# Two blocks of a transformer on one core: router, experts and overflow branch in one program, and two norms from one pass

## The reference, cut to what matters

```python
h = rmsnorm(x, norm_ffn) * (1 + scale_f) + shift_f
x = x + gate_f * hierarchical_moe(h, ...)     # 4 groups of 8 experts
x = rmsnorm(x, norm_final)                    # end of the first block
h = rms_norm(x, norm_mix_g) * (1 + sc1) + sh1 # start of the second

def hierarchical_moe(h, ...):
    g_logits = tok @ w_rg + b_rg              # best group, its softmax weight
    e_logits = tok @ w_re + b_re              # two best experts in that group
    combine = ...                             # weight of each expert for each token
    for e in range(32):
        hid = silu(tok @ w_gate[e]) * (tok @ w_up[e])
        out = out + combine[:, e:e + 1] * (hid @ w_down[e])
```

## Time and profile before

| | us |
|---|---|
| median of 3 runs | 1687.56 (1687.36 to 1689.58) |
| the profiled execution | 1686.78 |
| its span | 1685.1 |
| TensorE busy | 1523.9 (90%) |
| VectorE busy | 620.3 (37%) |
| ScalarE busy | 271.5 (16%) |
| GpSimd busy | 233.7 (14%) |
| mean granted clock of TensorE | 0.943 |
| moved by DMA | 352.37 MB |

### The profile page before, as it was taken

The page is one execution under the profiler, slowest core; times in us unless marked ns, Lnnn a source line. Parts: engine busy times, 40 slices in busy tenths (PEclk is TensorE's granted clock), DMA queues, the critical chain, the costliest instruction groups (busy, mean ns, idle before and its releaser), DMA issues. The chain is left out here.

```text
span 1685.1 us, 19200 instructions
## 1 busy us (share of the span) xinstructions
PE 1523.9 (90%) x7873; PEld 1168.5 (69%) x7873; DVE 620.3 (37%) x1089; ACT 271.5 (16%) x563; POOL 233.7 (14%) x305
## 2 busy tenths in 40 slices
PE   2999999498787489989999999899999998999997
PEld 2776775366454178867888888777776887777774
DVE  5577371522121245674445211233322962100002
ACT  1210120110000121121235300100001272100001
POOL 5054000000000110053344500300000000000000
PEclk7998998699999779999999999899999999999999
DMA  9874440499999847684675444788844411344440
GB/s 340 317 269 144 150 150 1 205 413 417 415 416 417 279 128 252 211 298 146 161 189 144 130 148 152 286 307 304 299 150 125 150 51 50 124 151 149 149 149 25
DMA packets 171998, 352.37 MB, mean 209 GB/s; under 512 B 6889, under 2 KB 134048, under 8 KB 154512
## 3 DMA queue, kind: packets, MB, share of 16 engines
q1 hardware_dynamic: 162784, 310.73, 51.5%
q0 software_dynamic: 9136, 40.55, 7.9%
HBM read 350.09 MB, written 1.16 MB: 208 GB/s over the span
## 5 line engine op out<-in xcount | busy, mean ns | idle before, releaser
L2368 PE MATMUL PS<-HT,ring 128*128 128x256 f32 x1616 | 352.5, 379 | 0.0
L2368 PEld LDWEIGHTS PS<-HT,ring 128*128 128x128 f32 x1616 | 307.0, 190 | 49.4 <-issue 8.6
L1688 PE MATMUL PS<-HT,ring 128*128 128x256 f32 x1152 | 265.5, 389 | 2.9 <-PEq L1546 2.9
L1688 PEld LDWEIGHTS PS<-HT,ring 128*128 128x128 f32 x1152 | 220.6, 194 | 40.1 <-issue 10.4
L2674 DVE TENSOR_TENSOR hid<-PS,silu 128x512 f32<-128x512 f32 x22 | 15.2, 692 | 359.0 <-PE PS L2368 359.0
L2384 PE MATMUL PS<-ring,hid 128*128 128x512 f32 x320 | 140.6, 592 | 0.0
L2384 PEld LDWEIGHTS PS<-ring,hid 128*128 128x128 f32 x320 | 60.8, 190 | 68.0 <-issue 67.0
L1847 PE MATMUL PS<-ring,y_T 128*128 128x256 f32 x384 | 83.3, 379 | 0.0
L1847 PEld LDWEIGHTS PS<-ring,y_T 128*128 128x128 f32 x384 | 72.9, 190 | 9.9
L2559 ACT ACTIVATE silu<-PS 128x512 f32<-128x512 f32 x22 | 13.1, 597 | 394.4 <-PE PS L2368 394.4
L426 DVE TENSOR_TENSOR expert_sums<-expert_sums,PS 128x1024 f32<-128x1024 f32 x16 | 19.5, 1222 | 139.9 <-PE PS L374 139.9
(11 more groups left out here) (528 smaller groups left out, 1852.3 us busy)
## 6 DMA issues: line engine op xcount, KB each, us to landing
ring<-in_hy_w_in SPq DMA_DIRECT2D x40, 1024.0 KB, 7.1
ada_stage<-in_ada_w POOLq DMA_DIRECT2D x24, 1024.0 KB, 5.9
ring<-in_ffn_w_gate SPq DMA_DIRECT2D x22, 1024.0 KB, 5.4
ring<-in_ffn_w_up SPq DMA_DIRECT2D x22, 1024.0 KB, 5.3
ring<-in_ffn_w_down SPq DMA_DIRECT2D x22, 1024.0 KB, 4.8
ring_extra<-in_expert_w_up SPq DMA_DIRECT2D x20, 1024.0 KB, 23.3
ring_extra<-in_expert_w_down SPq DMA_DIRECT2D x20, 1024.0 KB, 25.1
ring_extra<-in_expert_w_gate SPq DMA_DIRECT2D x20, 1024.0 KB, 19.9
```

Source lines behind the costliest of these rows:

```text
L1688: mm = pe.matmul(dst, w[:, k, half * P:(half + 1) * P], HT[:, k, :], start=(k == 0), stop=(k == KT - 1))
L2368: mm = pe.matmul(dst, w[:, k, m * P:(m + 1) * P], HT[:, k, :], start=(k == 0), stop=(k == KT - 1))
```

## The change

It merges the programs 3 to 7 into one and the norms of 8 into mixer 2's program, and it reorders the work in them.

- `clear_phase_sems` goes. GpSimd clears the semaphores of a phase in the program of the next one.
- SP runs RING items ahead of mixer 1 to its end; the merged program issues the final norm's gain (into `gate_a`) and then the other items.
- The router takes its logits from X before the norm: X is transposed, multiplied by router weights with the scale in them, then the reciprocal root is applied to the logits, and the product of shift and weights is added to the bias. Squares, root and the scaled rows `xn` are made beside that; HT with normed rows is not made any more (only in the overflow branch).
- `pick` is made for quad 0 first, the rest while TensorE gathers; turning `heavy` moves behind the gate products of quad 0.
- The rows of the experts are multiplied by `gate_b` as they leave PSUM (`gate_rows`, VectorE), and `add` adds to X. The last quad's scatter is cut in four pieces in four banks. `expert_sums` and the two products behind it go.
- The overflow branch stands at the end of the same program behind a flag that each engine loads.
- Four unused ScalarE operations on a few words (`idle`) name the function that is wanted next.
- Norms: `xg` = X times gain. The squares of X and of `xg` are summed one after the other and both roots are taken at once; rows are scaled once for mixer 2, and X is rescaled behind that. The transposes and evictions go to banks 4 to 7 in mixer 2's own program, and its first matmuls wait for one block each.
- `gate_a` is loaded later by GpSimd, behind its small loads and the clearing.

```diff
-    def clear_phase_sems():
-
-        with nc.Block() as block:
-            @block.gpsimd
-            def _(pool):
-                for _, s in phase_sems:
-                    pool.sem_clear(s)
-        for scope, _ in reversed(phase_sems):
+    def retire_sems():
+
+        old = list(phase_sems)
+        phase_sems.clear()
+        return old
+
+    def clear_retired(pool, old):
+        for _, s in old:
+            pool.sem_clear(s)
+
+    def release_sems(old):
+        for scope, _ in reversed(old):
             scope.close()
...
-                    send_until(sp, min(s + 1, segs["moe"].base - RING))
+                    send_until(sp, s + 1)
...
             @block.sync
             def _(sp):
-                send_until(sp, segs["moe"].base, RING + EXTRA)
+                sp.dma_start(fg[:], t["norm_final"].partition_broadcast(P)).then_inc(fg_in, 16)
+                send_until(sp, base, RING + EXTRA)
+                send_until(sp, segs["hy_x"].base)
...
             def _(pe):
-                pe.wait_ge(r_small, 96)
-                for i in range(TT):
-                    for k in range(KT):
-                        mm = pe.matmul(PS[:, i, 0:NR], HT[:, k, i * P:(i + 1) * P], wr[:, k, :],
+                for b in range(4):
+                    for i in range(TT):
+                        for k in (2 * b, 2 * b + 1):
+                            mm = pe.transpose(PS[:, 4 + b, (k % 2) * S + i * P:(k % 2) * S + (i + 1) * P],
+                                              X[:, i, :].rearrange("p (m k) -> p k m", k=KT)[:, k, :], ident[:])
+                    mm.then_inc(x_turned, 1)
...
+                pe.wait_ge(wr_ok, 1)
+                for k in range(KT):
+                    if k % 2 == 0 and k < 4:
+                        pe.wait_ge(xt_dve, k // 2 + 1)
+                    elif k % 2 == 0:
+                        pe.wait_ge(xt_act, k // 2 - 1)
+                    for i in range(TT):
+                        mm = pe.matmul(PS[:, i, 0:NR], XR[:, k, i * P:(i + 1) * P], wr_s[:, k, :],
                                        start=(k == 0), stop=(k == KT - 1))
-                mm.then_inc(lgm, 1)
+                mm.then_inc(made, 1)
+                pe.wait_ge(wr_ok, 2)
+                pe.matmul(PS[:, 2, 0:NR], ones[:], shift_sum[:], start=True, stop=True).then_inc(made, 1)
...
+                pe.wait_ge(normed, TT)
+                pe.wait_ge(picked, 1)
+                gather(0, 0)
+                gather(0, 1)
                 for q in range(QUADS):
-                    if q >= 4:
-                        pe.wait_ge(moved, q - 3)
+                    pe.wait_ge(hs_ready, q * 2 + 2)
+                    up_gate(0, q)
+                    if q:
+                        scatter(0, q - 1)
+                    else:
+                        pe.wait_ge(heavied, TT)
+                        turn_heavy()
+                    up_gate(1, q)
+                    if q:
+                        scatter(1, q - 1)
+                    if q < QUADS - 1:
+                        pe.wait_ge(picked, 2)
+                        gather(q + 1, 0)
+                    turn(q)
+                    if q < QUADS - 1:
+                        gather(q + 1, 1)
+                    if q == 0:
+                        pe.wait_ge(put_mv, QUADS)
+                    down(q)
+                pe.wait_ge(y_moved, QUADS)
+                pe.wait_ge(added, FINAL)
+                for i, h, bank in LAST_PIECES:
+                    pe.matmul(PS[:, bank, :], put[:, QUADS - 1, i * P:(i + 1) * P], ys[:, h * 512:(h + 1) * 512],
+                              start=True, stop=True).then_inc(scattered, 1)
...
+                act.activation(idle[:, 0:1], ident[:, 0:1], ACT.Sqrt)
+                for i in range(TT):
+                    act.activation(xn[:, i, :], X[:, i, :], ACT.Square, accum_out=stat[:, i:i + 1]).then_inc(squared, 1)
+                for b in range(2, 4):
+                    act.wait_ge(x_turned, b + 1)
+                    act.activation(XR[:, 2 * b:2 * b + 2, :], PS[:, 4 + b, :].rearrange("p (a n) -> p a n", a=2), ACT.Copy)\
+                        .then_inc(xt_act, 1)
+                act.wait_ge(meaned, 1)
+                act.activation(stat[:, 4:6], stat[:, 2:4], ACT.Sqrt).then_inc(rooted, 1)
+                act.activation(idle[:, 1:2], ident[:, 0:1], ACT.Exp)
...
+                dve.tensor_tensor(wr_s, wr[:], bc(scale, 2, NR), ALU.mult).then_inc(wr_ok, 1)
+                for b in range(2):
+                    dve.wait_ge(x_turned, b + 1)
+                    dve.tensor_copy(XR[:, 2 * b:2 * b + 2, :], PS[:, 4 + b, :].rearrange("p (a n) -> p a n", a=2))\
+                        .then_inc(xt_dve, 1)
+                step(dve.tensor_tensor(wr_t, wr[:], bc(shift, 2, NR), ALU.mult))
+                dve.tensor_reduce(shift_sum[:], wr_t.rearrange("p k n -> p n k"), AX.X, ALU.add).then_inc(wr_ok, 1)
+                dve.wait_ge(squared, TT)
+                dve.tensor_scalar(stat[:, 2:4], stat[:, 0:2], 1.0 / D, EPS, ALU.mult, ALU.add).then_inc(meaned, 1)
+                dve.wait_ge(rooted, 1)
+                step(dve.reciprocal(stat[:, 6:8], stat[:, 4:6]))
+                for i in range(TT):
+                    dve.tensor_scalar(xn[:, i, :], X[:, i, :], stat[:, 6 + i:7 + i], None, ALU.mult).then_inc(normed, 1)
+                dve.wait_ge(made, BIAS)
+                step(dve.tensor_tensor(br[:], br[:], PS[:, 2, 0:NR], ALU.add))
+                for i in range(TT):
+                    ins = dve.scalar_tensor_tensor(out=lg[:, i, :], in0=PS[:, i, 0:NR], scalar=stat[:, 6 + i:7 + i],
+                                                   in1=br[:], op0=ALU.mult, op1=ALU.add)
+                step(ins)
...
+                def choose(e0, e1):
+                    n = e1 - e0
+                    for i in range(TT):
+                        ins = dve.tensor_tensor(pick[:, i, e0:e1, :], bc(place[:, i, e0:e1], 2, SLOTS), bc(slot_no[:], 1, n),
+                                                ALU.is_equal)
+                    ins.then_inc(picked, 1)
+
+                choose(0, QUAD)
                 step(dve.tensor_reduce(most[:, 0:1], PS[:, 3, 0:EXPERTS], AX.X, ALU.max))
                 step(dve.tensor_scalar(most[:, 1:2], most[:, 0:1], float(SLOTS), None, ALU.is_gt))
-                dve.tensor_copy(some_left[:], most[:, 1:2])
+                dve.tensor_copy(some_left[:], most[:, 1:2]).then_inc(left, 1)
+                choose(QUAD, EXPERTS)
...
+                def gate_rows(q):
+                    dve.wait_ge(used, item(q, "d", QUAD - 1) + 1)
+                    dve.tensor_tensor(ys, PS[:, 4:6, :].rearrange("p b n -> p (b n)"), gate_b[:], ALU.mult)\
+                        .then_inc(y_moved, 1)
+
+                def add(h, q):
+                    dve.wait_ge(scattered, q * 2 + h + 1)
+                    part = X[:, :, h * 512:(h + 1) * 512]
+                    dve.tensor_tensor(part, part, PS[:, 6:8, :], ALU.add).then_inc(added, 1)
...
+                make_rows(0)
+                dve.wait_ge(picked, 2)
                 for i in range(TT):
-                    step(dve.tensor_tensor(pick[:, i], bc(place[:, i, :], 2, SLOTS), bc(slot_no[:], 1, EXPERTS),
-                                           ALU.is_equal))
                     dve.tensor_tensor(heavy[:, i], pick[:, i], bc(em[:, i, :], 2, SLOTS), ALU.mult).then_inc(heavied, 1)
-                dve.wait_ge(lgm, 2)
-                dve.tensor_copy(rest[:], PS[0:EXPERTS, 0, 0:S])
-        route.close()
-        sums = sb(scope, "expert_sums", [P, TT, D])
-        routed_experts(pick, put, xn, sums)
-        held.close()
-        overflow_experts(rest, rows_dram, some_left, sums)
-        with nc.Block() as block:
-            @block.vector
-            def _(dve):
-                step = stepper(dve, dve_step)
-                step(dve.tensor_tensor(sums[:], sums[:], bc(gate_b[:], 1, TT), ALU.mult))
-                dve.tensor_tensor(X[:], X[:], sums[:], ALU.add)
+                step(dve.tensor_scalar(keep[:], place[:], float(SLOTS), None, ALU.is_ge))
+                dve.tensor_tensor(keep[:], keep[:], em[:], ALU.mult)
+                for q in range(QUADS):
+                    if q:
+                        add(0, q - 1)
+                        add(1, q - 1)
+                    activate(q)
+                    if q < QUADS - 1:
+                        make_rows(q + 1)
+                    gate_rows(q)
+                dve.wait_ge(added, FINAL)
+                for n, (i, h, bank) in enumerate(LAST_PIECES):
+                    dve.wait_ge(scattered, FINAL + n + 1)
+                    part = X[:, i, h * 512:(h + 1) * 512]
+                    ins = dve.tensor_tensor(part, part, PS[:, bank, :], ALU.add)
+                ins.then_inc(go, 1)
...
+                clear_retired(pool, retired)
+                pool.wait_ge(left, 1)
+                with if_some(pool):
...
+                        if s == 0 and q < 2:
+                            if k < KT // 2:
```

(42 more changed lines are left out.)

572 lines of the change are left out of this document (233 added, 339 removed).

## The result

The changed kernel takes **1650.16 us** (median of 4, 1645.73 to 1653.31), the kernel before 1688.57 in the same session (1687.36 to 1691.79): ratio 0.9768, 95% interval 0.974 to 0.9796. The forecast was 1654, with a range of 1646 to 1663. The profiled execution took 1651.4 us with a span of 1649.4, against 1686.78: 35.4 us less, where the sum of the terms was 33.1.

What follows compares the result with a forecast made beforehand. The expert stage was taken as bound by its weight stream, restarted when the router lets quad 0's gate products end. 18.3 + 9.1 + 3.0 + 3.0 - 0.3 = 33.1 us off 1686.78 gave 1653.7, forecast 1654, range 1646 to 1663.

Steps and rivals of the forecast that it cites:

- up to the start of the merged program: Mixer 1: early items share SP's queue with the last two modulation fetches; 0.3 us lost, 2.5 at worst.
- shift of the stage: Expert stage: earlier gate products of quad 0 let the weight stream flow from 338.5 instead of 356.8; 18.3 us gained.
- tail, from its end: From the last down product's end to the next program's first square: 7.9 us instead of 17.0; 9.1 gained.
- first operation to scaled rows: Norms ahead of mixer 2: first square to scaled rows takes 5.3 us instead of 8.3; 3.0 gained.
- scaled rows to in-projection, and what follows up to 575 us: Mixer 2's start: first in-projection matmul 2.8 us earlier, plus 0.2 for the clock; 3.0 gained.
- second hole: Expert stage: rival that a later down(0) starves the stream again; 1657 at 6 us late, chance 0.07.
- 14.7 later: Router: issue of item 16, after quad 0's gate products, follows the gather's start by 14.7 us, as before.
- 1.5 us for a slow clock: Gather behind a cold stretch of TensorE: taken as 1.5 us slower, bounds 0 and 2.
- 335 at most: Weight stream: first 16 items and the final gain are in by 335 us at most; then it stands still.
- The rival had a tenth: Behind 600 us: a stall of VectorE, ScalarE and GpSimd at about 725 us loses gain; 1660, chance 0.10.
- slower than reckoned: Router: rival that TensorE's clock stays at half through the logits and the gather is at its bound; 1657, chance 0.15.
- The rival of more than reckoned: Gather at full rate, load behind the add, blocks without a gap: 1651, or 1647 if clock stays up; chance 0.10.

Runs made afterwards that it cites:

- the run with the clearing: Changed kernel with the two clearings of semaphores back in programs of their own, all engines waiting: 1660.0 us, ratio 0.9832.
- an execution of the kernel before with the same mixer 2: Kernel before with only SP's limit in mixer 1 lifted, so six expert items are fetched early: 1688.68 us, ratio 1.0001.
- one with the short router: Changed kernel without the square root named ahead of the overflow branch, so both ways leave Silu's table: 1647.63 us, ratio 0.9754.
- the kernel with the adds spread: Changed kernel with the sixteen adds of the modulation sums one in a step, instead of two in some steps: 1638.58 us, ratio 0.9703.
- the root named in mixer 2: Changed kernel with an unused square root at the head of ScalarE's list in mixer 2's program, ahead of the squares: 1645.09 us, ratio 0.9746.

## Why the prediction was right, and where its terms were off

The kernel is faster by what the forecast named, but the sum is closer than its terms. By the spans of the profiled pair, in us:

| term | forecast | measured |
|---|---|---|
| up to the start of the merged program | -0.3 | 1.9 |
| shift of the stage | 18.3 | 23.3 |
| last down product | 0 | 0.3 |
| tail, from its end | 9.1 | 10.4 |
| first operation to scaled rows | 3.0 | 0.8 |
| scaled rows to in-projection, and what follows up to 575 us | 3.0 | 6.0 |
| mixer 2, up to 1060 us | 0 | -9.2 |
| behind it | 0 | 2.2 |
| sum | 33.1 | 35.7 |

The two times differ by 35.4. At 575 us the lead was 42.7 us, nearly ten more than forecast; that the profiled pair came within 3 us of the forecast at its end is luck, as mixer 2 gave 9.2 back in that execution. The medians are 38.4 apart, and 41.2 in the last session.

- **Shift of the stage.** The mechanism was right in each point: the gate products of quad 0 set the restart (the run with the clearing: 7.8 us at item 16, 7.7 at the last down product), the early items only have to be early enough, and no second hole came. The size was off: TensorE's work up to item 16 is 5.4 us shorter than reckoned. Of that, 2.2 lie ahead of the gather (transposes and logits), 1.5 are the gather and 1.7 the gate products, 3.67 from their start to the issue instead of the 5.36 that lay in the "14.7 later" carried over from before (5.20 in the run with the clearing). For transposes and gate products it is the clock, at 1.00 in the changed kernel and at 0.50 for much of them before; I had taken it for the transposes' own pace that they took 3.67. For the gather it isn't: I charged 1.5 us for a slow clock, the clock was slow (0.50 for over four us), and it cost nothing. And the stream was done with its 16 items 30 us after the start and not 33, the forecast's "335 at most", so that it hardly had to wait.
- **Tail.** 1.3 us more than the 9.1. The last adds follow each other at 0.86 us (546.00, 546.86), and from the last one's end to the next program there are 0.7 us, where the forecast had 1.75 for flag, jump and border: 1.0 of the 1.3. The flag's load is hidden, which the forecast had left open. Its pieces up to the last add (1.3 + 4.0 + 0.69) also sum to 6.0 and not to the 6.1 that it gives; 5.9 were measured.
- **Norm.** Right in the arithmetic (5.4 without loads), wrong in the sum: the forecast put the table loads at nothing and didn't ask which table ScalarE holds behind a branch. Two loads of 1.28 us cost 2.1, and 0.8 of the 3.0 us were won.
- **First matmuls.** 7.2 became 4.3, as forecast (4.4). The clock gave 1.8 us, not the 0.2 that I took out of 1.5 at most: 40 records in 8.80 us, 10.56 before.
- **Is anything lost behind 600 us?** The rival had a tenth, and the profiled pair looked like it, with 9.2 us given back. It isn't a fixed loss by the change: an execution of the kernel before with the same mixer 2 loses nearly as much, and one with the short router loses 0.2. The medians, 38.4 us apart, speak against it too. A loss of up to 3 us isn't excluded. The forecast also missed a stall: its "only short stall" before 1053 us, 5.1 us, has a second one beside it in the trace of before, 1.1 us for `rows_q`, and both grew in the profile of the changed kernel.
- **The other rivals.** The clock was at 0.50 in the first part of the gather, but no work in the router's stretches was slower than reckoned. The rival of more than reckoned (1651) came nearest to the median: the load hides behind the add, the gather costs nothing more, and the clock stays up from mixer 1.

What is not settled: why the clock falls where it does, why the gather doesn't feel it, why two executions of one kernel wait 1 or 5 us for `rows_q`, and what part of the 1.9 us ahead of the merged program is the change's; 2.7 us were there at 186 us, ahead of every edit, and are the execution's.

## What to carry to other kernels

A prefetch and the release of its slots are one term: alone the early items were worth nothing, with the short router 8 to 10 us. A pause between programs can cost its length and then the lower clock of what follows (3.8 us and 3.4 more in the run with the clearing), so a step's duration taken from behind a pause isn't the step's own. If one way through a branch ends with another ScalarE table than the other, loads stand behind it; end both with the same one. Before a loss in a stretch that wasn't edited is explained, look at a second execution of the old kernel there: one trace of each can differ by more than the effect.

## What the runs showed of the hardware

- A border of 1.78 us of rest left TensorE's clock at 1.00, and 16 transposes took 2.04 us; after a rest of 5.58 us it was 0.50, and they took 3.65. The length of the rest alone doesn't decide: in the kernel before, a rest of 1.83 us ahead of the logits, behind only 3.68 us of transposes and 9.23 of rest ahead of those, was followed by a fall to 0.50 at 317 us, with TensorE at work.
- The gather of 32 records took 7.86 to 7.89 us whether its clock was 1.00 throughout or 0.50 in its first half.
- The clock also fell to 0.76 to 0.87 in stretches of mixer 2 in which TensorE was busy all 20 us (740 to 760), in the kernel with the adds spread too, where it waits nowhere near:

```profile
720.00:740.00 20.00, 20.00 (x88) 14.84 (x88) 9.16 (x18) 3.40 (x7) 6.43 (x7) 0.91 0.41 130
740.00:760.00 20.00, 20.00 (x89) 15.78 (x88) 7.12 (x18) 3.38 (x7) 5.38 (x6) 0.83 0.19 54
```

- A table load took 1.28 us, and the next ScalarE operation started 0.01 us behind it (548.62 and 549.91 with the root named in mixer 2). "ScalarE: Activation LUTs", What ACT_TABLE_LOAD costs, of the Trainium skill gives 1283 ns for the load, with which the trace agrees, and about 1380 ns more for a drain, 2.66 us for every switch; here two loads cost 2.1 us in all, and no drain shows.
- The weight stream moved 389 GB/s in the first 15 us of its program, while VectorE was busy for 10.7 of them, TensorE for 7.5 and ScalarE for 6.8, and 417 in the next 15. Before, with VectorE busy for 6.0, TensorE for 7.9 and ScalarE for 1.6, it had moved 381 in its first 15: no loss shows from the router's work beside it.
